# Squares of the residual on ScalarE and VectorE, and the seven-product weights in four batches: a two-layer trunk in float32

## The reference, cut to what matters

```python
def rms_norm(x, g):
    xf = x.astype(jnp.float32)
    y = xf * lax.rsqrt(jnp.mean(xf * xf, axis=-1, keepdims=True) + EPS)
    return (y * g.astype(jnp.float32)).astype(x.dtype)

def swiglu_ffn(h, w_gate, w_up, w_down):
    return (jax.nn.silu(h @ w_gate) * (h @ w_up)) @ w_down

for i in range(DEPTH):
    ...
    x = x + y
    h = rms_norm(x, norm_ffn_g[i])
    x = x + swiglu_ffn(h, ffn_w_gate[i], ffn_w_up[i], ffn_w_down[i])
return rms_norm(x, final_norm_g)
```

## Time and profile before

| | |
|---|---|
| Median of 3 runs | 1129.05 us (1128.79 to 1130.07) |
| The profiled execution's own time | 1129.93 us |
| Its span | 1128.1 us |
| TensorE busy | 1081.5 us, 96% |
| VectorE busy | 865.8 us, 77% |
| ScalarE busy | 477.3 us, 42% |
| GpSimd busy | 233.4 us, 21% |
| DMA | 101.68 MB, mean 90 GB/s |

### The profile page before, as it was taken

One profiled execution on the slowest core, in us unless ns is written; L12 is line 12 of the kernel. 1 busy time (PEld: TensorE's weight loads), 2 busy tenths in 40 slices (PEclk: granted clock), 3 DMA queues, 4 the chain that ended last, 5 costly groups with the idle time before them and its releaser, 6 DMA issues. The chain is left out here.

```text
span 1128.1 us, 19245 instructions
## 1 busy us (share of the span) xinstructions
PE 1081.5 (96%) x6630; PEld 955.8 (85%) x6630; DVE 865.8 (77%) x1332; ACT 477.3 (42%) x820; POOL 233.4 (21%) x179
## 2 busy tenths in 40 slices
PE   9999997899999999999999989967999999999997
PEld 7888886799999998888877756757999999988887
DVE  5755568899999997444587899388999999973443
ACT  6222233545445544222355466235554545452222
POOL 6000014333233320111200000143322333201110
PEclk9999999799999999999999999998999999999999
DMA  6333422123323333334232011021332233333321
GB/s 197 105 93 93 128 58 75 64 88 110 112 88 114 110 99 108 99 102 114 94 93 75 1 38 38 1 74 43 108 112 94 92 112 111 102 114 103 95 71 75
DMA packets 144040, 101.68 MB, mean 90 GB/s; under 512 B 3912, under 2 KB 142336, under 8 KB 144000
## 3 DMA queue, kind: packets, MB, share of 16 engines
q1 hardware_dynamic: 143648, 100.61, 29.1%
q0 software_dynamic: 320, 0.55, 0.2%
q10 hardware_dynamic: 32, 0.01, 0.0%
HBM read 99.06 MB, written 2.10 MB: 90 GB/s over the span
## 5 line engine op out<-in xcount | busy, mean ns | idle before, releaser
L375 PE MATMUL ps<-x_op_hi,op_w_hi 128*128 128x256 f32 x1232 | 353.7, 287 | 23.9 <-DVE x_op_lo L1019 22.6
L376 PE MATMUL ps<-x_op_lo,op_w_hi 128*128 128x256 f32 x1232 | 350.8, 285 | 0.0
L377 PE MATMUL ps<-x_op_hi,op_w_lo 128*128 128x256 f32 x1232 | 350.6, 285 | 0.0
L375 PEld LDWEIGHTS ps<-x_op_hi,op_w_hi 128*128 128x128 f32 x1232 | 238.7, 194 | 27.9 <-DVE x_op_lo L1019 23.2
L376 PEld LDWEIGHTS ps<-x_op_lo,op_w_hi 128*128 128x128 f32 x1232 | 238.9, 194 | 0.6 <-issue 0.5
L377 PEld LDWEIGHTS ps<-x_op_hi,op_w_lo 128*128 128x128 f32 x1232 | 238.7, 194 | 0.0
L375 PE MATMUL ps<-hid_hi,wgt_hi 128*128 128x512 f32 (+1 forms) x550 | 212.3, 386 | 4.2 <-DVE wgt_lo L359 4.2
L359 DVE TENSOR_TENSOR wgt_lo<-raw,wgt_hi 128x1024 fp32r<-128x1024 f32 (+4 forms) x131 | 137.7, 1066 | 101.9 <-ACT wgt_hi L350 100.4
L377 PE MATMUL ps<-hid_hi,wgt_lo 128*128 128x512 f32 (+1 forms) x550 | 210.0, 382 | 0.0
L376 PE MATMUL ps<-hid_lo,wgt_hi 128*128 128x512 f32 (+1 forms) x550 | 209.9, 382 | 0.0
L350 ACT ACTIVATE wgt_hi<-raw 128x1024 fp32r<-128x1024 f32 (+4 forms) x131 | 107.0, 831 | 151.0 <-PE ps L377 149.4
(11 more groups left out here) (161 smaller groups left out, 1321.2 us busy)
## 6 DMA issues: line engine op xcount, KB each, us to landing
pair_raw<-in_ffn_w_gate SPq DMA_DIRECT2D x22, 1024.0 KB, 5.1
pair_raw<-in_ffn_w_up SPq DMA_DIRECT2D x22, 1024.0 KB, 5.2
raw<-in_conv_w_in SPq DMA_DIRECT2D x24, 512.0 KB, 3.8
raw<-in_ffn_w_down SPq DMA_DIRECT2D x32, 384.0 KB, 3.2
raw<-in_ffn_w_down SPq DMA_DIRECT2D x32, 320.0 KB, 2.9
raw<-in_conv_w_out SPq DMA_DIRECT2D x8, 512.0 KB, 3.7
raw<-in_mla_w_o SPq DMA_DIRECT2D x8, 512.0 KB, 3.8
x_nat<-in_x SPq DMA_DIRECT2D x4, 512.0 KB, 7.1
```

The costliest lines, as they stand in the source:

```text
L375: nc.tensor.matmul(acc, wh, xh, start=first, stop=False)
L376: nc.tensor.matmul(acc, wh, xl, start=False, stop=False)
L377: return nc.tensor.matmul(acc, wl, xh, start=False, stop=last)
```

## The change: what it does

In the mixers' output stages the squares leave GpSimd. ScalarE squares each tile right behind its scaled copy (tile 0 straight into `sq_sum`, which is then not cleared), and VectorE adds the square of tiles 1 to 7 to `sq_sum`. On odd tiles but the last VectorE now prepares weights ahead of the two `x_op_lo` steps, not behind them. GpSimd goes to the weight sums at once. The squares at the start of the program and in the down stages stay with GpSimd.

The seven weight parts come in four batches: part 0; parts 1 to 3 in one operation of 1536 elements; part 5; parts 4 and 6 in one of 1024. Each product waits for its batch (`READY`). GpSimd's sums of a set wait for four parts of the set before, where they waited for two and three. On VectorE the `hid_lo` split moves ahead of `u2`, batch 1 comes behind `u2` and batch 3 behind the last sums; in up groups but the last, `u2` is one operation of 512 elements in place of two of 256.

```diff
+        def part_of(par, part):
+            b = blocks(par)
+            if part == 0:
+                return slice(0, 1), b["A11"].unsqueeze(1)
+            if part == 1:
+                return slice(1, 4), w_sum[:, 0:3, :].rearrange("p n (c m) -> p n c m", m=P)
+            if part == 2:
+                return slice(5, 6), w_sum[:, 3:4, :].rearrange("p n (c m) -> p n c m", m=P)
+            return slice(4, 7, 2), pair_raw[:, par, 1:DC:2, :].rearrange("p c (n m) -> p n c m", m=P)[:, ::-1]
+
+        PART_SIZE, PART_DONE, USED_BEFORE = [1, 3, 1, 2], [1, 4, 5, 7], [1, 4, 6, 7]
+        READY = [1, 4, 4, 4, 7, 5, 7]
...
+        def make_op_hi(eng, l, i, par, part):
+            if part in (0, 3):
                 wait(eng, pair_in[par], i * 16 + 16 * (PAIRS_F * l + 1))
             else:
+                wait(eng, sum_done, i * 4 + (4 * PAIRS_F * l + 2 * par + 2))
+                wait(eng, sum_ve, i * 4 + (4 * PAIRS_F * l + 2 * par + part))
+            slots, src = part_of(par, part)
+            nc.scalar.activation(four(op_w_hi[:, slots, :]), src, ACT.Copy).then_inc(op_hi, PART_SIZE[part])
+
+        def make_op_lo(eng, l, i, par, part):
+            wait(eng, op_hi, op_no(l, i, par, 0) + PART_DONE[part])
+            slots, src = part_of(par, part)
+            nc.vector.tensor_tensor(four(op_w_lo[:, slots, :]), src, four(op_w_hi[:, slots, :]).bitcast(F32),
+                                    ALU.subtract).then_inc(op_lo, PART_SIZE[part])
...
             def weight_sums(l, i, par):
-                if not isinstance(free, int) or free > 0:
-                    wait(pool, op_lo, free + 2)
+                if not isinstance(free, int) or free >= 0:
+                    wait(pool, op_lo, free + 4)
                     wait(pool, sum_done, done)
...
-                    wait(pool, op_lo, free + 3)
+                    wait(pool, op_lo, free + 4)
...
                 if n % 2:
-                    with pool.Fori(0, DC // 2) as m:
-                        add_square(n, m, tile_free, m + (T0[name] + 1))
                     weight_sums(n // 2, 0, 0)
-                    with pool.Fori(DC // 2, DC) as m:
-                        add_square(n, m, tile_free, m + (T0[name] + 1))
                     ffn(n // 2)
...
+                    if m > 1:
+                        wait(sc, sq_added, squares_before(2 * l + 1) + m)
+                    nc.scalar.activation((sq if m else sq_sum)[:, :], xT[:, m, :],
+                                         ACT.Square).then_inc(sq_new if m else sq_added, 1)
                     if m % 2 == 0:
                         x_op_hi_of(l, c, 0, 0, 2)
...
+                    def add_square():
+                        if m:
+                            n0 = squares_before(2 * l + 1)
+                            ve.wait_ge(sq_new, SQ_NEW[l] + m)
+                            ve.wait_ge(sq_added, n0 + m)
+                            nc.vector.tensor_tensor(sq_sum[:, :], sq_sum[:, :], sq[:, :], ALU.add).then_inc(sq_added, 1)
...
                         weights()
+                        add_square()
                         x_op_lo_of(l, c, 0, 0, 2)
                     else:
...
+                        if m < DC - 1:
+                            weights()
                         x_op_lo_of(l, c, 1, 2, 4)
+                        add_square()
                         x_op_lo_of(l, c, 2, 4, 7)
-                        weights()
+                        if m == DC - 1:
+                            weights()
...
                     weights(0)
                     if nxt is not None:
                         third_sum(*nxt)
-                    weights(1)
-                    if nxt is not None:
                         fourth_sum(*nxt)
-                    weights(2)
-                    weights(3)
+                    if split and par == 0:
+                        wait(ve, h_hi, i * 2 + FC * l)
+                        nc.vector.tensor_tensor(hid_lo[:, ds(i * 2 - 2, 2), :], hid[:, ds(i * 2 - 2, 2), :],
+                                                hid_hi[:, ds(i * 2 - 2, 2), :].bitcast(F32), ALU.subtract).then_inc(h_lo, 2)
                     wait(ve, op_used, op0 + 5)
...
+                    elif par:
+                        u_2 = quarters[:, ds(i * 4 + 4, 1), :].rearrange("p a n -> p (a n)")
+                        nc.vector.tensor_tensor(quarters[:, ds(i * 4 + 3, 2), :], halves, twice, ALU.add).then_inc(u2_done, 1)
...
-                    weights(4)
+                    weights(1)
                     wait(ve, u2_done, g + 1)
...
-                    weights(5)
+                    weights(2)
                     if first and par == 0:
                         make_inv(ve, n_inv)
                     wait(ve, op_used, op0 + 7)
...
-                    weights(6)
+                    weights(3)
...
-                    wait(pe, op_lo, op_no(l, i, par, p) + 1)
+                    wait(pe, op_lo, op_no(l, i, par, 0) + READY[p])
```

More of the change, by code:

```diff
@@ L429, in trunk_kernel @@
         ROOT = {0: 0, 1: 1, 2: 2, 3: 5, 4: 6}
+        SQ_NEW = [X_POOL, X_POOL + 2 * DC - 1]
         def statistic(norm):
@@ L497, in op_ready, with four @@
+        PART_SIZE, PART_DONE, USED_BEFORE = [1, 3, 1, 2], [1, 4, 5, 7], [1, 4, 6, 7]
+        READY = [1, 4, 4, 4, 7, 5, 7]
+        def four(part):
+            return part.rearrange("p n (c m) -> p n c m", m=P)
+        def make_op_hi(eng, l, i, par, part):
+            if part in (0, 3):
                 wait(eng, pair_in[par], i * 16 + 16 * (PAIRS_F * l + 1))
             else:
-                made, n = {1: (sum_done, 1), 2: (sum_done, 2), 3: (sum_ve, 1), 5: (sum_ve, 2)}[p]
-                wait(eng, made, i * 4 + (4 * PAIRS_F * l + 2 * par + n))
@@ L720, in out_body @@
                         sc.wait_ge(w_used, U0[name] + 4 + u + 1)
-                        for p in range(2 * u, min(2 * u + 2, OPS)):
-                            make_op_hi(sc, l, 0, 0, p)
+                        make_op_hi(sc, l, 0, 0, u)
             out_body("conv_out", 0)
@@ L742, in group @@
                     nc.scalar.activation(s1[:, :], ps[:, 4 * par, 0:N], ACT.Copy).then_inc(s1_done, 1)
-                    weights(0)
-                    wait(sc, op_used, op0 + 2)
-                    weights(1)
+                    if nxt is not None:
+                        make_op_hi(sc, *nxt, 0)
+                    else:
+                        wait(sc, op_used, op0 + 2)
+                        unit_hi(sc, f"down{l}", 0, 0)
                     if par:
@@ L752, in group @@
                                              ACT.Copy).then_inc(h_hi, 2)
-                    for p in range(2, OPS):
-                        wait(sc, op_used, op0 + p + 1)
-                        weights(p)
-                        if first and par == 0 and p == 3:
+                    for part in range(1, 4):
+                        wait(sc, op_used, op0 + USED_BEFORE[part])
+                        if nxt is not None:
+                            make_op_hi(sc, *nxt, part)
+                        elif part < 3:
+                            unit_hi(sc, f"down{l}", 0, part)
+                        if first and par == 0 and part == 1:
                             make_root(sc, n_root, D)
@@ L1000, in fourth_sum @@
                 wait(ve, sum_done, i * 4 + (4 * PAIRS_F * l + 2 * par + 2))
-                wait(ve, op_lo, op_no(l, i, par, 0) - OPS + 6)
+                wait(ve, op_lo, op_no(l, i, par, 0) - OPS + 5)
                 nc.vector.tensor_tensor(wide(w_sum, 3), blocks(par)["A12"], wide(w_sum, 1), ALU.subtract).then_inc(sum_ve, 1)
@@ L1070, in group, with weights @@
                     to = pair if par else gate
-                    def weights(p):
+                    def weights(part):
                         if nxt is not None:
-                            make_op_lo(ve, *nxt, p)
-                        elif p % 2:
-                            unit_lo(ve, f"down{l}", 0, p // 2)
+                            make_op_lo(ve, *nxt, part)
+                        elif part < 3:
+                            unit_lo(ve, f"down{l}", 0, part)
                     weights(0)
@@ L1104, in group @@
                                                 hid_hi[:, ds(i * 2 - 2, 2), :].bitcast(F32), ALU.subtract).then_inc(h_lo, 2)
+                    wait(ve, op_used, op0 + 5)
+                    wait(ve, s1_done, g + 1)
+                    halves = ps[:, b0 + 1, :].rearrange("p (h n) -> p h n", h=2)
+                    twice = s1[:, :].unsqueeze(1).broadcast_to([P, 2, N])
+                    if par and last:
+                        u_2 = u2
+                        nc.vector.tensor_tensor(pair[:, 3, :], halves[:, 0, :], s1[:, :], ALU.add)
+                        nc.vector.tensor_tensor(u2, halves[:, 1, :], s1[:, :], ALU.add).then_inc(u2_done, 1)
+                    elif par:
+                        u_2 = quarters[:, ds(i * 4 + 4, 1), :].rearrange("p a n -> p (a n)")
```

(10 more changed lines are left out.)

44 lines of the change are left out of this document (6 added, 38 removed).

## The result

The changed kernel takes 1139.23 us (median of 4 runs, 1138.30 to 1140.16), the kernel before 1129.56 in the runs beside it (4 runs, 1128.79 to 1131.57). The ratio is 1.0079, with a 95% interval of 1.0067 to 1.0092. The profiled span is 1138.2 us, 10.1 longer than before.

A forecast was written before the change was run, and what follows sets the result against it. TensorE sets the end wherever fed, so only time it lacks operands counts. Layer 0 3.7 + 1.5 + 0.8 = 6.0, layer 1 3.7 + 1.5 - 0.5 = 4.7, together +10.7: forecast 1139.8 us, range 1136 to 1144.

The forecast's parts named there:

- Output stages, +3.7 each: First and second mixer's output stages: TensorE's stall at the end was to end 3.7 us later in each layer.
- R+2.9: Output stage, tile 0: `wgt_lo` was to run from 2.9 us after R, the start of the tile's residual.
- Square at nothing: Output stages: ScalarE's new Square, 0.61 us, was to fit behind the scaled copy and cost nothing; uncovered, at most 8 us.
- The copy and batch of 1536: Parts 1 to 3 merged: ScalarE's copy was put at 1.50 us, VectorE's operation at 1.67, both extrapolated.
- Product 4 of group 1, 1.5 each: Seven-product stage: product 4 waits for the last batch, behind the reciprocal; a new TensorE stall of 1.5 us per layer.
- The loop, +0.8 and -0.5: Five `split` pairs at 20.65 us against TensorE's 20.16: +0.8 us in layer 0, -0.5 in layer 1.
- The lock: VectorE operations with both inputs in SBUF wait for GpSimd's running operation to end, then take their own time less about 0.13.
- Rival 2: GpSimd's sums hit only VectorE operations that read PSUM, so stages, first groups and loops gain: 1124.3 us; chance 0.08.
- (1): Loop: merging parts saves the whole fixed part per start, 0.15 us, so the loop's loss goes: 1134.9 us; chance 0.15.
- (3): Loads later than 5.1 us make sums hold batch 3 and the gate product: 1152 us at worst, 1146 halfway; chance 0.17.
- (4): Output stages: what the squares' waits give back pays for odd tiles' idle time; within 2.3 us of 1129.05; chance 0.05.

The follow-up runs named there:

- e3_order: The changed kernel with the weights behind both `x_op_lo` steps again on every odd tile, the add between those steps; 1119.29 us, ratio to before 0.9911.
- e5_small_sums: The changed kernel with GpSimd's weight sums cut to 8 of 128 columns, except in each layer's first group; 1128.85 us, ratio to before 0.9985.
- e6_late_inv: The changed kernel with the reciprocal of the norm (`make_inv`) moved behind the last batch of weight parts, `weights(3)`; 1139.09 us, ratio to before 1.0076.

## Why the prediction was right, step by step

The forecast was 1139.8 us; 1139.23 came out, and +10.7 on the profiled execution was +10.1 in the span. Every term of the sum came within 0.25 us, so it was not luck: no error paid for another.

- **Output stages, +3.7 each.** Measured, at the end of the stall, +3.6 in layer 0 (202.83 to 206.41) and, less the 5.96 brought along, +3.5 in layer 1 (at the start of group 1, 3.5 and 3.25). By tile: 5.30, 7.83, 7.85, 7.82, 4.94, 10.99 and, in tile 6 until `x_op_lo` starts, 4.31; foretold 5.27, 7.82, 8.1, 7.82, 4.9, 11.0, 4.3. Only tile 2 was off, by 0.25. Its two waits came as foretold, in the weight step (2.08) and the add (1.77), but somewhat shorter than 1.1 each. For tile 0 the prediction has `wgt_lo` run from R+2.9, which doesn't fit its own 5.27; it ran from R+3.55, which does. Shown by experiment: the delay needs the new order (`e3_order`), and 2.0 of it is the lock in tile 5 (`e5_small_sums`).
- **Square at nothing.** Right: 0.61 us, and nothing on ScalarE waits for it. The cover had 0.30 us to spare on odd tiles and none on even ones.
- **The copy and batch of 1536.** 1.47 and 1.67 from start to start (216.94 to 218.61), for 1.50 and 1.67.
- **Product 4 of group 1, 1.5 each.** Measured 1.44 in both layers at the gap, 1.54 over the group; batch 2 took 1.50, as foretold with 0.9 of waiting. `e6_late_inv` corrects the cause: with the reciprocal out of the way the loss stays, one group on.
- **The loop, +0.8 and -0.5.** Measured +1.0 and -0.6. Pairs in the steady part take 20.62 us, foretold 20.65. Its waits came as foretold as well: batch 2 takes 1.48 (0.8 of waiting for 0.9), batch 3 1.38 (0.17 for 0.2), batch 1 of the up group waits 0.5 for ScalarE (for 0.4), and with GpSimd's sums cut short nothing is lost.
- **The lock.** It was a reading of four rows, and on it rested tile 5, batch 2 and the loop. Rival 2, with the sums out of the way, had a price of 1124.3; when they were cut, 1128.85 came. Most of the 4.5 us between is tile 2: `e5_small_sums` leaves the sums of each layer's first group whole, and these cost the weight step and the add 0.85 and 1.09 us (2.08 and 1.77 against 1.23 and 0.68), 3.9 over both stages.

The rivals: (1) merging saves the whole fixed part: refuted. A batch of 1536 holds VectorE for 1.67 us from start to start, three parts of 512 for 1.80, so 0.06 to 0.07 per saved start. The Trainium skill (VectorE: DVE Perf Modes, section on the TRN2 errata) gives a fixed latency of about 150 cycles per instruction with SBUF sources; in a single duration (0.68 for 512 elements) the trace has it, in a queue it doesn't. (2) Refuted in its condition, see above. (3) Late loads: in layer 0 it happened once. GpSimd waited for a load, its second sum came late, and the up product met it:

```profile
253.19 1.74 POOL L620 TENSOR_TENSOR w_sum<-pair_raw 128x512 f32<-128x512 f32 x1 [7.48 <-DMA pair_raw<-in_ffn_w_up]
255.94 2.31 DVE L1140 TENSOR_TENSOR hid<-hid,gate_u 128x1024 f32 x1
```

This step takes 1.21 elsewhere, and TensorE's group there took 10.83 in place of 10.54, 0.3 us more. One pair of ten is far from the rival's price. (4) Tile 5 at 8 us: it took 10.99.

What the prediction did not see: how much the change left unused. It priced each edit where it was put, found +10.7, and never asked what the squares' way would bring with the steps in another order. It is 20 us in `e3_order`, of which 2.6 stand at the clock in its trace.

## What to carry to other kernels

On the engine that carries the longest chain, put every step that waits for another engine's copy behind steps that are ready, and look at what its semaphore releases next: a batch that frees GpSimd to run beside steps that share the lock with it costs twice, by its own wait and by theirs. A merged step saves 0.06 us per start here, but its last consumer sets the due time for all of it, so merge only parts that are due together. And price a removal by itself (cut the work to a few columns) before judging the kernel that carries it: here 14 us were there to be had in the old order, and the kernel that did it was 10 slower.
